# Half of the tokens of an expert layer computed densely over streamed units, the other half added row by row on VectorE

## The reference, cut to what matters

```python
q = (hf @ w_q).reshape(T, 8, 2, 128)                      # 8 heads, 2 halves
s = einsum('thpd,hpnd->thpn', q, sub_keys)                # 128 keys in each half
sc, idx = top_k(s, 16)                                    # best 16 in each half
cand = sc[..., 0, :, None] + sc[..., 1, None, :]          # 16 x 16 pairs
eidx = the 16 best pairs, as idx_first * 128 + idx_second # 16 experts for each head
gate = softmax(their scores)
act  = gelu(dot(u_tab[eidx], h))                          # 8 x 16 = 128 experts for each token
y    = sum(gate * act * v_tab[eidx])                      # 128 rows of 1024 for each token
h    = h + g2 * y
return rms_norm(h, final_g)
```

## Time and profile before

| | us |
|---|---|
| time, median of 3 runs (3455.7 to 3457.72) | 3456.01 |
| span of the profiled execution | 3452.1 |
| last matmul on `bank` ends, from the span's start | 3442.8 |
| first gather is issued, from the span's start | 2132.36 |

### The profile page before, as it was taken

The page is one execution under the profiler, slowest core; times in us unless marked ns, Lnnn a source line. Parts: engine busy times, 40 slices in busy tenths (PEclk is TensorE's granted clock), DMA queues, the critical chain, the costliest instruction groups (busy, mean ns, idle before and its releaser), DMA issues.

```text
span 3452.1 us, 34902 instructions
## 1 busy us (share of the span) xinstructions
PE 3142.6 (91%) x12254; PEld 2099.6 (61%) x12254; DVE 2087.5 (60%) x3701; ACT 1062.6 (31%) x2577; POOL 1917.9 (56%) x1198
## 2 busy tenths in 40 slices
PE   7999999999999999999999999999978787777776
PEld 5778778887766888868777677544433333333332
DVE  5764453336764433479556776777667676666654
ACT  4564441112165211120132432333333332333222
POOL 4545259997403899968767565444444444434432
PEclk9999999999999999999999999999999999999999
DMA  4430022232311222323413124999999999999997
GB/s 164 171 134 1 13 86 98 97 120 74 134 62 49 90 95 96 115 71 124 140 62 115 50 80 172 421 421 419 422 415 412 421 421 421 421 421 420 421 421 299
DMA packets 108994, 741.68 MB, mean 215 GB/s; under 512 B 11816, under 2 KB 12968, under 8 KB 20776
## 3 DMA queue, kind: packets, MB, share of 16 engines
q0 software_dynamic: 73728, 536.90, 37.5%
q1 hardware_dynamic: 31488, 196.25, 16.2%
q10 hardware_dynamic: 3624, 6.56, 0.5%
HBM read 731.28 MB, written 8.39 MB: 214 GB/s over the span
## 4 chain that ended last, share of the span: by engine, by line
PE 63%; DMA 21%; DVE 8%; ACT 4%; issue 2%; POOL 2%; DVEq 0%; POOLq 0%; ACTq 0%
DMA arena<-in_peer_uv,rstd 15%; PE bank L1298 13%; PE bank L1299 13%; PE bank L1300 13%; PE bank L1814 8%; DMA weight_ring<-in_peer_uv,rstd 3%; DMA normed<-in_peer_uv,rstd 2%; DVE arena L3295 2%; PE bank L1829 1%; PE bank L1744 1%; PE bank L1726 1%; PE bank L1612 1%; PE bank L1490 1%; PE bank L1245 1%; PE bank L1500 1%
## 5 line engine op out<-in xcount | busy, mean ns | idle before, releaser
L1155 POOL DMA_INDIRECT arena<-in_peer_uv,rstd x419 | 456.4, 1089 | 622.0 <-PE bank L1814 570.3
L3295 DVE CUSTOM_DVE_ANT_0 arena<-arena,branch 128x1024 f32<-128x1024 f32 x419 | 510.5, 1225 | 333.5 <-DMA arena<-in_peer_uv,rstd 327.5
L1300 PE MATMUL bank<-split_arena 128*128 128x512 f32 x1776 | 695.1, 391 | 0.0
L1066 POOL TENSOR_TENSOR split_arena<-weight_ring,ones 128x1024 fp32r<-128x1024 f32 x204 | 506.6, 2483 | 151.0 <-PE bank L1300 99.3
L1298 PE MATMUL bank<-split_arena 128*128 128x512 f32 x1392 | 546.6, 393 | 5.6 <-DVE split_normed L2697 2.5
L1299 PE MATMUL bank<-split_arena 128*128 128x512 f32 x1392 | 542.3, 390 | 0.0
L1068 POOL TENSOR_TENSOR split_arena<-weight_ring,split_arena 128x1024 fp32r<-128x1024 f32 x204 | 519.3, 2545 | 16.0
L1814 PE MATMUL bank<-arena,row_diagonals 128*128 128x512 f32 x836 | 397.8, 618 | 92.0 <-ACT row_diagonals L2425 91.7
L1814 PE MATMUL bank<-arena,level_mask 128*128 128x512 f32 x840 | 392.0, 608 | 75.0 <-ACT level_mask L2425 74.7
L1300 PEld LDWEIGHTS bank<-split_arena 128*128 128x128 f32 x1776 | 334.0, 188 | 73.6
L1035 POOL TENSOR_TENSOR split_arena<-weight_ring,split_arena 128x1024 fp32r<-128x1024 f32 x54 | 129.5, 2406 | 401.2 <-ACT split_arena L1980 349.3
(11 more groups left out here) (490 smaller groups left out, 4921.4 us busy)
## 6 DMA issues: line engine op xcount, KB each, us to landing
weight_ring<-in_w_up SPq DMA_DIRECT2D x32, 1024.0 KB, 4.9
weight_ring<-in_w_down SPq DMA_DIRECT2D x32, 1024.0 KB, 4.9
weight_ring<-in_w_in SPq DMA_DIRECT2D x32, 1024.0 KB, 5.0
weight_ring<-in_ada_w SPq DMA_DIRECT2D x24, 1024.0 KB, 4.9
weight_ring<-in_w_in_a SPq DMA_DIRECT2D x12, 1024.0 KB, 6.4
weight_ring<-in_w_out SPq DMA_DIRECT2D x12, 1024.0 KB, 6.9
weight_ring<-in_w_in_b SPq DMA_DIRECT2D x10, 1024.0 KB, 5.9
arena<-in_peer_uv,rstd POOLq DMA_INDIRECT x419
```

The costliest lines, as they stand in the source:

```text
L1066: pool.tensor_tensor(hi, part, bc_mid(ones[:], DT), ALU.mult).then_inc(split_hi, 1)
L1155: pool.indirect_dma_start(row_slots[slot_of[r]], None, a["peer_uv"], bass.IndirectOffsetOnAxis(ap=experts[n % 2][:, c:c + 1], axis=0)).the ...
L1300: return pe.matmul(psum[t.bank][:], hi, a_lo[k], start=False, stop=last)
L3295: dve.tensor_tensor_reduce(row, row, h_tok[:, r // NE, :], 1.0, 0.0, ALU.mult, ALU.add, dots[:, i % 4, j:j + 1]).then_inc(dot_ready, 1)
```

## The change

Rows are kept for the lower two blocks only (tokens 0 to 255: 256 rows). For the upper 256 tokens the layer is computed over all 16384 experts:

* Two new tables hold u and v in 128 units of 512 KB each (4 KB in each partition). Unit j has the 128 experts whose second key is j. SP streams the 256 units (items) through four places in `residual`, whose content is first stored in DRAM and later loaded back to `normed`.
* `up_unit`: 8 matmuls of 256 columns (128 experts x 256 tokens, summed over 1024), whose Gelu ACT writes into `weights` (64 units at a time, in `arena`). `down_unit`: 4 matmuls of 512 columns that add `weights` times v to four PSUM banks over all 128 units.
* Between them the Gelus are multiplied with the gates. For a group of 8 tokens, `one_hots` on DVE (one instruction of 128x1024 and four of 128x128) and `second_ones` on POOL (four of 128x128) write matrices of ones at the picked keys, one of them times the gate; `gate_products` on PE multiplies them (16 matmuls of 64 columns); `gate_weights` on DVE multiplies the first 64 units' gates into `weights`; ACT stores the other 64 units' gates in DRAM (`keep_gates`), from where they come back for `later_weights`.
* The order is a list of 296 steps: 64 up items; 32 gate steps; 128 items, down (0 to 63) and up (64 to 127) in turn; 8 "back" steps (four `later_weights` each); 64 down items (64 to 127).
* A row's dot (`dot_row`, DVE) and its weight (`weigh_row`, ACT: Gelu, then times the gate) stand in one step, and DVE adds it at the start of the next (`add_row`, one instruction of 128x1024 that multiplies with the weight and adds to a sum in SBUF). PE and the diagonals are out of it. The rows are dealt over the steps: 64 in the first 64 steps (from step 3), 10 in the gate steps, 120 in the 128 items, 2 in the back steps, 60 in the first 58 of the last steps. They have 10 places of 8 KB, of which four are in use from the start and given up from step 24 on, and the others open from step 23 on.
* The searches run in another order: blocks 0, 2 and 3 (93 pieces) in the first 61 steps, two pieces in each of the steps 12 to 43 and one in the others; block 1 (32 pieces) in steps 98 to 129.
* The scaling of the upper three blocks (`scale_input(others)`, L3144) moves on DVE from behind the first group's rows to ahead of the search of head 0, and `shift(others)` on ACT stands ahead of the steps.

The diff, cut to its core:

```diff
-NROW = TT * NE
+NROW = 2 * NE
+DENSE = 2 * P
+WHALF = NKEY // 2
+GTOK = 8
+NGATE = DENSE // GTOK
+LOADS = 4
+RAWS = 4
+RING8 = 8
...
+        STEPS = [("item", n) for n in range(WHALF)] + [("gate", q) for q in range(NGATE)]
+        STEPS += [("item", n) for n in range(WHALF, 3 * WHALF)]
+        STEPS += [("back", i) for i in range(NGATE // LOADS)]
+        STEPS += [("item", n) for n in range(3 * WHALF, 4 * WHALF)]
...
@@ SP
+            sp.dma_start(x_dram, X[:, :, :]).then_inc(x_saved, 16)
+            def load_item(n):
+                value, m = ITEMS[n]
+                if n < RAWS:
+                    if n == 0:
+                        sp.wait_ge(x_saved, 16)
+                        sp.wait_ge(scaled_ready, 2 * DT)
+                else:
+                    sp.wait_ge(item_done, n - RAWS + 1)
+                sp.dma_start(raws[n % RAWS], a["peer_vd" if value else "peer_ut"][m]).then_inc(raw_landed[n % RAWS], 16)
+            for n in range(len(ITEMS)):
+                load_item(n)
...
+                elif n == 2 * WHALF:
+                    for q in range(LOADS):
+                        load_gates(q)
+                elif n == 3 * WHALF + RAWS - 1:
+                    for q in range(LOADS, NGATE):
+                        load_gates(q)
+                    sp.dma_start(H[:, :, :], x_dram).then_inc(x_back, 16)
...
@@ POOL
+            def gather(r):
...
+                i, before = row_place[r], row_before[r]
+                if before is not None:
+                    pool.wait_ge(row_added, before + 1)
...
+                for x in range(GTOK // 2, GTOK):
+                    m = pool.tensor_scalar(one_second[q % 2][:, x, :], iota_key, index_t[b][:, 1, at:at + 1],
+                                           index_t[b][:, 2, at:at + 1], ALU.is_equal, ALU.mult)
...
@@ PE
-                    for t, c in zip(row_sums[n], (0, 512)):
-                        m = pe.matmul(psum[t.bank][:], diag[i % 2][:, j, :], row_slots[slot_of[r]][:, D + c:D + c + 512],
...
+            def up_unit(n, j):
+                t = u_tiles[j]
+                unit_landed(n)
+                free(pe, t)
+                for k in range(DT):
+                    m = pe.matmul(psum[t.bank][:, 0:DENSE], blk(raws[n % RAWS], k), H[:, k, DENSE:], start=k == 0, stop=k == DT - 1)
+                m.then_inc(item_done, 1)
+            def down_unit(n, m):
+                unit_landed(n)
...
+                elif m == WHALF:
+                    pe.wait_ge(gate_used, NGATE)
+                for b in range(2):
+                    for c in range(2):
+                        x = pe.matmul(psum[2 * b + c][:], blk(weights[:, m % WHALF, :], b), raws[n % RAWS][:, 512 * c:512 * (c + 1)],
+                                      start=m == 0, stop=m == NKEY - 1)
+                x.then_inc(item_done, 1)
+            def gate_products(q):
...
+                for x in range(GTOK):
+                    for half, t in enumerate(gate_tiles[q]):
+                        m = pe.matmul(psum[t.bank][:, x * WHALF:(x + 1) * WHALF], one_first[q % 2][:, x, :],
+                                      one_second[q % 2][:, x, half * WHALF:(half + 1) * WHALF], start=True, stop=True)
...
@@ ACT
+            def activate(j):
...
+                full(act, t)
+                act.activation(weights[:, j % WHALF, :], psum[t.bank][:, 0:DENSE], ACT.Gelu).then_inc(bank_out[t.bank], 1)
+            def weigh_row(r):
...
+                act.wait_ge(row_dot, r + 1)
...
+                act.activation(w, dots[:, r % RING8:r % RING8 + 1], ACT.Gelu).then_inc(row_gelu, 1)
+                act.wait_ge(row_gelu, r + 1)
+                act.activation(w, w, ACT.Copy, scale=gates[n][:, c:c + 1]).then_inc(row_weight, 1)
...
@@ DVE
+            def one_hots(q):
...
+                dve.tensor_tensor(one_first[q % 2], bc_mid(iota_key, GTOK), bc_last(index_t[b][:, 0, GTOK * t:GTOK * (t + 1)], NKEY),
+                                  ALU.is_equal)
...
+            def dot_row(r):
...
+                dve.wait_ge(row_landed[row_place[r]], 16 * row_fill[r])
+                dve.tensor_tensor_reduce(row, row, h_tok[:, n, :], 1.0, 0.0, ALU.mult, ALU.add,
+                                         dots[:, r % RING8:r % RING8 + 1]).then_inc(row_dot, 1)
+            def add_row(r):
...
+                dve.wait_ge(row_weight, r + 1)
...
+                    m = dve.scalar_tensor_tensor(row_acc[n], row, w, row_acc[n], ALU.mult, ALU.add)
...
+            for s, (kind, v) in enumerate(STEPS):
+                if kind == "gate":
+                    one_hots(v)
+                    if v:
+                        gate_weights(v - 1)
+                elif kind == "back":
+                    for q in range(LOADS * v, LOADS * (v + 1)):
+                        later_weights(q)
...
+                for r in rows_at[s - 1] if s else ():
+                    add_row(r)
+                for r in rows_at[s]:
+                    dot_row(r)
...
+                for k in piece_at.get(s, ()):
+                    next(walks[k], None)
+            add_rows(2)
+            finish_rows(0)
+            finish_rows(1)
+            add_rows(3)
+            finish_rows(2)
+            finish_rows(3)
```

More of the change, by code:

```diff
@@ L557, in build @@
[L557 to L573, removed]
+        first_at = {8: 5, 17: 6, 18: 7}
@@ new lines, in build @@
+        piece_count = {}
+        search_steps = []
+        for s in range(61):
+            search_steps += [s] * (2 if 12 <= s < 44 else 1)
+        search_steps += range(MIX_AT + 2, MIX_AT + 2 + 64)
+        piece_at, search_end, at = {}, {}, iter(search_steps)
+        for n, g in SEARCHES[1:]:
+            for _ in range(PIECES if parts[n][g][1] == 2 else 5):
+                search_end[n, g] = next(at)
+                piece_at.setdefault(search_end[n, g], []).append((n, g))
+        exp_at = {e + 1: k for k, e in search_end.items()}
@@ L576, in build @@
+        v_tiles = [item_tile(2 * NKEY - 1, b) for b in range(4)]
         q_f = region(0, LH)
@@ L1139, in _ @@
                 split_half(u, h, out_w, ((landed[u.slot], 16 * u.load), place), u.own + h + 1)
-            for r in range(NROW):
+            def gather(r):
                 n, c = divmod(r, NE)
@@ new lines, in _ @@
+            for s, (kind, v) in enumerate(STEPS):
+                if kind == "gate":
+                    gate_products(v)
+                elif kind == "item" and ITEMS[v][0]:
+                    down_unit(v, ITEMS[v][1])
+                elif kind == "item":
+                    up_unit(v, ITEMS[v][1])
+                if s in first_at:
+                    for h in range(2):
+                        first_half(first_at[s], h)
+                if s in query_at:
+                    query_piece(*query_at[s])
+                if s in turn_at:
+                    token_turn(*turn_at[s])
+                if s in score_at:
+                    key_scores(*score_at[s])
+                if s in index_at:
+                    b = index_at[s]
+                    pe.wait_ge(turn_in, sum(k[0] >= 2 and searched[k] <= searched[2 + b, 3] for k in SEARCHES))
+                    turn(index_tiles[b], [firsts[2 + b], seconds[2 + b], gates[2 + b]])
+                if s == GAIN_AT:
@@ new lines, in _ @@
+            for s, (kind, v) in enumerate(STEPS):
+                if s and STEPS[s - 1][0] == "item" and not ITEMS[STEPS[s - 1][1]][0]:
+                    activate(ITEMS[STEPS[s - 1][1]][1])
+                if s == 1:
+                    gate_exp(0, 0)
+                if s - 1 in first_at:
+                    take_first(first_at[s - 1])
+                if s - 1 in query_at and query_at[s - 1][1] % 2:
+                    take_rest(query_at[s - 1][0], query_at[s - 1][1] // 2)
+                if s - 1 in turn_at:
+                    n, x = turn_at[s - 1]
+                    take(tok_turns[n][x], h_tok[:, n, 512 * x:512 * (x + 1)])
+                if s - 1 in score_at:
+                    take_scores(*score_at[s - 1])
+                if s - 1 in index_at:
+                    b = index_at[s - 1]
+                    take(index_tiles[b], index_t[b].rearrange("p a n -> p (a n)"), width=3 * NKEY)
+                if s and STEPS[s - 1][0] == "gate":
+                    keep_gates(STEPS[s - 1][1])
+                if s in exp_at:
+                    gate_exp(*exp_at[s])
+                for r in rows_at[s]:
+                    weigh_row(r)
+                if s == GAIN_AT + 1:
@@ L3280, in _ @@
             first_ids()
+            scale_input(others)
             for _ in search(0, 0):
                 pass
[L3284 to L3311 removed]
```

570 lines of the change are left out of this document (344 added, 226 removed).

## The result

| | before | after |
|---|---|---|
| median, us | 3456.86 (3455.7 to 3457.97, 4 runs) | 3542.86 (3541.8 to 3544.56, 4 runs) |
| span of the profiled execution, us | 3452.1 | 3541.7 |
| ratio | | 1.025, 95% 1.0236 to 1.0265 |

The change makes the kernel 2.5% slower; the forecast was 3408 us, 1.4% faster. The page of the kernel after: PE, granted clock and DMA in 40 slices, the two queues, and the largest groups of the new work.

A forecast was written before the change was run, and what follows sets the result against it. The kernel was taken as bound by DMA's gathers from 2132 us to the end. Stages, each at its slowest engine, 2146 + 369 + 128 + 482 + 34 + 230 + 15, gave 3404, plus 3.9 us 3408 us; range 3335 to 3485.

The forecast's parts named there:

- The step that failed: Gate steps: PE's 32 records of 64 columns take 2.9 to 3.6 us, under DVE's 3.7 us a step.
- the +99: Gate steps with what is before them: forecast 128 us, measured 227.3, the largest difference by stage.
- the 0.2 us a step: Gate steps: added to DVE's 3.7 us because POOL's work may hold up DVE's compare, giving 3.9 us a step.
- Start: Before step 0: scaling ends near 2136 us, a unit lands in 4.1 us, PE's first up item starts at 2146.
- Steps 0 to 63: 64 up items, 64 rows, 93 query pieces: 369 us, paced by PE up to step 11, then DVE.
- A row: DVE's cost of a gathered row, dot 1.15 and adding 1.25 us: 2.4 us (2.3 to 2.75).
- The first rival: DVE's rows are dearer and set the pace everywhere; at 3.4 us a row about 3545 us; chance 0.17.
- Mixed: 128 mixed items, 120 rows: 32 searching steps at 4.25 us, 96 at 3.6 us, 482 us in sum.
- Back: Back steps: PE waits while the last 28 gate loads return four at a time, 34 us (30 to 50).
- Last items: Last 64 down items: PE at 3.44 us each plus 9 us of turning, 230 us, DVE and DMA lying beside.
- The faster rival: All stages: steps couple better than thought and PE's pace rules, 3300 us; chance 0.15.
- Starving items: Mixed stage: items starve behind gathers at 3.75 us each, with slower gate returns 45 us more, 3453; chance 0.1.

The follow-up runs named there:

- e8_twice: The changed kernel with ten extra matmuls filling PE's gap before the first gate group and each group's 32 records issued twice: 3548.24 us (one run).
- e1_wide: The changed kernel with 14 of the 16 matmuls of a gate group covering 128 columns instead of 64: 3477.78 us, ratio 1.0057 to the kernel before.
- e7_wide_split: e1_wide with DVE making six and POOL two of a group's eight second one-hots, instead of four each: 3454.92 us, ratio 0.9996 to the kernel before.
- e6_three: The changed kernel with one 128-column matmul a token, ACT making three first one-hots, second ones split DVE five, POOL three: 3443.34 us, ratio 0.9963 to the kernel before.
- e5_no_gap: The changed kernel with ten unused 512-column matmuls filling PE's gap before the first gate group: 3539.39 us, ratio 1.0244 to the kernel before.
- e3_merged: The changed kernel with one 128-column matmul a token instead of two of 64, 16 records a group: 3483.51 us, ratio 1.0082 to the kernel before.

## Why the prediction was wrong

**The step that failed** is "PE has 32 records of 64 columns; their pace lies between one-column ones, (0.50 - 0.23) / 3 = 0.09, and 128-column ones, 0.11: 2.9 to 3.6 us." Both of its ends are rows at 2.4 GHz, and the forecast names no clock for the new stage. At the high clock the upper end is right: 0.112 us in e8_twice. In the change the pace was 0.213, all 32 steps long, and 32 x 6.83 us is 219 where 125 was written. With one 7.7 us gap where 3 us were allowed, that is the +99. None of its rows' durations warned of it, but the forecast itself had DVE at 3.9 us a step and PE at 2.9 to 3.6, so PE would wait in each step. The clock of such a stage should have been bounded too, at twice the price.

**A second size, hidden by the first.** "POOL's four short operations are each some 0.3 us or more" went by a row of another operation. They are 1.20 us on average. The timeline of POOL in one step after (DVE's compare, 1.22 us, starts at 2606.64):

```profile
2606.11 0.79 POOL L1293 TENSOR_SCALAR branch<-arena,masks 128x128 f32<-128x128 f32 x1 [0.51 <-PE bank L2044]
2606.89 1.73 POOL L1293 TENSOR_SCALAR branch<-arena,masks 128x128 f32<-128x128 f32 x1
2608.60 0.86 POOL L1293 TENSOR_SCALAR branch<-arena,masks 128x128 f32<-128x128 f32 x1
2609.45 0.79 POOL L1293 TENSOR_SCALAR branch<-arena,masks 128x128 f32<-128x128 f32 x1
```

It is 0.79 us alone (the last one), and 1.73 for the one beside DVE's compare. The forecast feared that POOL would hold up DVE's compare (the 0.2 us a step, and 165 us as a bound). It was the other way: DVE's compares took 1.218 us on average, as long as the 1.2 estimated for one alone, and POOL's was stretched. The Trainium skill, "SBUF — State Buffer", section "Who interferes with whom", has it that a DVE instruction with two SBUF inputs and a GpSimd one that reads SBUF exclude each other for a whole instruction, and that the order of issue decides who blocks. The stretch of 0.9 us agrees with that on POOL's side. The order of issue doesn't show here: DVE's compare began 0.25 us before POOL's first one ended, and was not lengthened.

**Of the 99 us**, e1_wide gives back 65 by the clock alone; its step is then POOL's, 4.94 us. The rest, 34 us, is POOL's and the balance of the engines: e7_wide_split gives back 23 more (21 by the ratios) and e6_three, at 4.0 us a step, another 12. With the gate steps at the 4 us of the forecast the kernel takes 3443 us, 0.4% less than before: inside the stated range, but 35 us over the forecast's 3408. In the change itself the other terms add 38 us:
- Start: the first up item came 5 us late. The scaling ended at 2140.4 us instead of 2136, PE had other work until 2147.6, and then waited 3.6 us for the first unit, which started its item 10.8 us after the unit's issue, beside gathers and three more units (DMA share 0.98), where 4.1 was taken. Steps 0 to 63: 372 us for 369, with DVE 91% busy in the first stretch above, as forecast. PE's records fill 95% of it where 85% was written.
- A row: dot 1.22, adding 1.28 us by its record (the next instruction starts 1.19 us after it), for which 1.25 was taken between 1.15 and 1.58. The first rival (dearer rows) gives nearly the measured number, 3545, and isn't what happened: its place, DVE, had 88 us of waiting in the gate steps.
- Mixed: the first 32 items, with searches, took 122 us for 136 (PE ran ahead of DVE), the other 96 took 373 for 346. DMA's rate was as forecast: the 401 GB/s of the stretch above is a mean over 416 to 418 in most of it and two holes, and at 417 an item and 0.94 rows are 3.62 us, where 3.65 was written. What was left out is mainly the holes. Near 2890 us PE waited 4.3 us for ACT, and at 3000 us 12.5 us for one unit, behind which DVE, POOL and then the transfers stood still. This unit was issued at 2988.2, right behind the first four gate loads (1 MB from 2984.9 on), and landed 24 us later, where 11 us is the median. No run moved these loads, so that they delayed it is likely and not shown. The PE timeline's row, and the busy time there and behind it:

```profile
3012.00 6.70 PE L2017 MATMUL bank<-normed,residual 128*128 128x256 f32 x16 [12.53 <-DMA residual<-in_peer_ut]
3005.00:3045.00 40.00, 33.00 (x107) 22.57 (x108) 18.67 (x23) 5.07 (x20) 11.52 (x8) 0.84 0.86 339
3045.00:3085.00 40.00, 39.48 (x132) 24.18 (x131) 23.94 (x31) 6.70 (x26) 16.32 (x10) 1.00 1.02 416
```

- Back: 41.4 us for 34 (30 to 50 given). DVE waited for gate loads, 13.3 us for those to `mem_keys` alone.
- Last items: 242 us for 230. PE is busy for 225 of 228 us, but the first 32 records, behind the back steps, took 16.5 us, not 13.8: the clock was 0.52 in the gap ahead. The other 9 us are DMA's, which the forecast let lie beside. From 3353 to 3458 us DMA is full, and 28 items start 3.76 us apart, not 3.44; one item and one row are 1.573 MB, 3.77 us at 417 GB/s. The busy time, and what PE's weight loads waited for in it:

```profile
3353.00:3458.00 105.00, 103.19 (x229) 40.53 (x227) 69.69 (x85) 13.92 (x56) 28.11 (x28) 1.00 1.02 417
PEld bank L2032 <- DMA residual<-in_peer_vd: 23.5, 27, 0.9
```

- The faster rival (3300) is excluded: with PE's clock restored, DVE and POOL set the gate steps and DMA the mixed ones. Starving items (3453) came true in part. The forecast's own sign of being wrong, that PE waits for landed units, did show: over the whole run the weight loads waited 60.7 us for units of u and 49.0 us for units of v. But all that cost 12 us in the mixed items and 7 in the back steps, where the rival had 29 and 16, and some 9 in the last ones, where it had none.

**What stays open.** That the clock fell because of waits among narrow matmuls rests on e5_no_gap and e8_twice, one kernel each; a 64-column stage whose waits alone are varied was not run, and e8_twice doubles the work besides taking the waits away. Why the clock held through e1_wide's waits and went up and down in e3_merged isn't settled either. The late unit at 3000 us was located, and its cause not tested.

## What to carry to other kernels

When a stage is made of a new kind of matmul, ask first which clock it will have, and write down both sums: the factor is two, more than most of the other bounds here. Filling each matmul's columns cost no time (0.112 us a record at 64 columns and at 128), and with 32 such records a group the clock was 0.99. The columns alone are no guarantee: with 16 of them a group (e3_merged) it was 0.70. And read a stage's rate in short stretches before calling it a rate: 401 GB/s was 417 with two holes. Last, price each helper engine's operation by a row of the same operation, or bound it upwards: the one taken at 0.3 us was 0.8 alone and 1.2 in company.

## What the runs showed of the hardware

- PE busy by its records is no promise of the high clock: 212.4 of 213 us busy at a granted clock of 0.50 in the change, with 64-column matmuls, and 159.1 of 160 us busy at 1.00 in e8_twice, with the same ones. With 128 columns, 32 records a group and waits of 1.1 to 1.9 us in each step it was 0.99 (e1_wide), with 16 records a group and waits up to 5.0 us 0.70 (e3_merged). The Trainium skill, "TensorE: Matmul & The Clock Gate", section "What's actually happening", says that "the default state is throttled, and activity releases the throttle"; the trace agrees for e1_wide, where the clock was back within a group after the 7.7 us gap, and in the change 213 us of busy records didn't release it.
- The pace of such short f32 matmuls follows the clock and not the columns: 0.112 us a record at 2.4 GHz for 64 columns (7.15 / 64) and for 128 ((3.74 - 0.27) / 31 in e1_wide, with 0.27 for one record), 0.213 at 1.2 GHz for 64. A weight load's record is 192 ns and 333 ns at the two levels, and the loads are busy as long as the matmuls (158.5 and 159.1 of 160 us in e8_twice), so the pace is probably theirs; no run varied the loads alone.
- DMA, full with gathers of 1 MB and loads of 512 KB together, moved 417 GB/s (3353 to 3458 us), against 421 with gathers alone. A 512 KB load took 11.3 us to land in it (median), against 4.1 for one in the kernel before.
